# Per-head mean squares from split operands, placement of the parts by transfers, and a later recurrence in a one-layer hybrid decoder block

## The reference

```
h = rmsnorm(x, norm_g);  proj = h @ w_in          # split into u, z, q, k, v, gates ...
y_lru: causal conv of u, gates r, i; a = exp(-8 r softplus(-lam)); b = sqrt(1-a^2) i xc
       h_t = a_t h_(t-1) + b_t;  y_lru = h * silu(z)
y_nsa: q (8 heads), k, v (2 heads): compressed, selected and window branches, sigmoid gates, * silu(z)
y_fox: 8 heads, softmax(q k / 8 + c_t - c_s) v, c = cumsum(log sigmoid(forget)), * silu(z)
       (every q and k is first RMS-normed over its 64 channels:
        q * rsqrt(mean(q*q over the head) + 1e-6) * gain)
out = x + concat(y_lru, y_nsa, y_fox) @ w_out
```

## Time and profile before

| | |
|---|---|
| median of 3 runs | 423.2 us (422.87 to 423.55) |
| the profiled execution, its own time | 423.57 us |
| its span, first to last instruction | 421.8 us |
| TensorE clock granted | full in the whole span |
| busy: PE, PEld, DVE, ACT, POOL | 413.2, 325.5, 285.7, 261.4, 62.5 us |
| projection of u to vn, of zl | about 9 to 107 us, 107 to 137 us |
| first attention stage | 137 to 206 us |
| fq to zn | 206 to 297 us |
| second attention stage | 297 to 337 us |
| zf and output projection | 329 to 422 us |

### The profile page before, as it was taken

The page is one execution under the profiler, slowest core; times in us unless marked ns, Lnnn a source line. Parts: engine busy times, 40 slices in busy tenths (PEclk is TensorE's granted clock), DMA queues, the critical chain, the costliest instruction groups (busy, mean ns, idle before and its releaser), DMA issues.

```text
span 421.8 us, 6567 instructions
## 1 busy us (share of the span) xinstructions
PE 413.2 (98%) x2234; PEld 325.5 (77%) x2234; DVE 285.7 (68%) x616; ACT 261.4 (62%) x519; POOL 62.5 (15%) x122
## 2 busy tenths in 40 slices
PE   8999999999999899999999999999799999999996
PEld 7876788779888766666677987988576688888885
DVE  4667759988998876766378756699777389422205
ACT  5846996687465887886088778771888554322200
POOL 3000000000000666564000000000466100000000
PEclk9999999999999999999999999999999999999999
DMA  8923534420313000000421234437710115731005
GB/s 283 343 78 101 165 99 113 135 68 35 101 51 102 0 2 1 2 1 2 135 86 55 101 82 121 124 109 167 198 33 2 51 59 196 278 101 66 2 0 199
DMA packets 14017, 40.51 MB, mean 96 GB/s; under 512 B 1928, under 2 KB 2184, under 8 KB 13728
## 3 DMA queue, kind: packets, MB, share of 16 engines
q1 hardware_dynamic: 13552, 39.51, 29.8%
q10 hardware_dynamic: 432, 0.58, 0.4%
HBM read 32.17 MB, written 2.10 MB: 81 GB/s over the span
## 4 chain that ended last, share of the span: by engine, by line
PE 77%; DVE 14%; issue 3%; ACT 2%; POOL 1%; SPq 1%; DMA 1%; POOLq 0%; DVEq 0%; ACTq 0%
PE bank L1425 10%; PE bank L1427 10%; PE bank L1426 10%; PE bank L1610 6%; PE bank L1591 6%; PE bank L1701 5%; PE bank L1700 5%; PE bank L1699 5%; PE bank L1581 3%; PE bank L1582 3%; PE bank L1500 2%; DVE wl L1000 2%; PE bank L1632 2%; PE bank L1398 2%; PE bank L1400 2%
## 5 line engine op out<-in xcount | busy, mean ns | idle before, releaser
L1425 PE MATMUL bank<-xh,wh 128*128 128x512 f32 x240 | 99.6, 415 | 0.0
L1427 PE MATMUL bank<-xh,wl 128*128 128x512 f32 x240 | 93.8, 391 | 0.0
L1426 PE MATMUL bank<-xl,wh 128*128 128x512 f32 x240 | 93.7, 390 | 0.0
L1000 DVE TENSOR_TENSOR wl<-raw,wh 128x1024 fp32r<-128x1024 f32 (+1 forms) x50 | 60.0, 1204 | 37.0 <-ACT wh L611 36.8
L611 ACT ACTIVATE wh<-raw 128x1024 fp32r<-128x1024 f32 (+1 forms) x50 | 51.6, 1037 | 30.4 <-PE bank L1701 25.9
L1425 PEld LDWEIGHTS bank<-xh,wh 128*128 128x128 f32 x240 | 45.1, 188 | 14.8 <-issue 5.4
L1224 DVE CUSTOM_DVE_ANT_0 bank<-bank,mask_row 128x256 f32<-128x256 f32 (+3 forms) x96 | 46.6, 499 | 13.4 <-PE bank L1582 13.2
L1426 PEld LDWEIGHTS bank<-xl,wh 128*128 128x128 f32 x240 | 45.1, 188 | 11.3 <-issue 2.6
L1427 PEld LDWEIGHTS bank<-xh,wl 128*128 128x128 f32 x240 | 45.0, 188 | 9.7
L588 POOL TENSOR_SCALAR probs<-probs,rcp,gates 128x384 f32<-128x384 f32 (+3 forms) x44 | 26.5, 613 | 135.4 <-DVE rcp L1244 135.3
L792 ACT ACTIVATE probs<-bank,negmax 128x256 f32<-128x256 f32 (+3 forms) x64 | 33.7, 530 | 6.2 <-DVE negmax L1224 5.9
(11 more groups left out here) (246 smaller groups left out, 769.1 us busy)
## 6 DMA issues: line engine op xcount, KB each, us to landing
raw<-in_w_in SPq DMA_DIRECT2D x35, 512.0 KB, 3.3
raw<-in_w_out SPq DMA_DIRECT2D x12, 512.0 KB, 3.4
x_raw<-in_xT SPq DMA_DIRECT2D x8, 256.0 KB, 6.1
x_res<-in_x_tok SPq DMA_DIRECT2D x1, 2048.0 KB, 10.1
out_y<-y_out SPq DMA_DIRECT2D x8, 256.0 KB, 2.1
raw<-in_w_in SPq DMA_DIRECT2D x3, 384.0 KB, 3.3
cmp_w_sb<-in_cmp_w SPq DMA_DIRECT2D x1, 1024.0 KB, 5.6
kh_fox<-kh_fox SPq DMA_DIRECT2D x8, 128.0 KB, 2.3
```

The lines of the kernel that those rows point to most:

```text
L1000: dve.tensor_tensor(wl[:, c % HL, cols], raw[:, c % RAW, cols], wh[:, c % HL, cols].bitcast(F32), ALU.subtract).then_inc(wl_ready, 1)
L1425: pe.matmul(dst, hi, xh[:, k, :], start=(k == 0), stop=False)
L1426: pe.matmul(dst, hi, xl[:, k, :], start=False, stop=False)
L1427: mm = pe.matmul(dst, lo, xh[:, k, :], start=False, stop=(k == KT - 1))
```

## The change

1. **Head means.** ACT copies the squares to an fp32r plane (its high part), DVE makes the low part in a second plane (`square_low`), and PE multiplies both by an fp32r block matrix (`block_r`), two fast matmuls instead of one fp32 product. The bank alternates. The place of the product moves from the middle of the next chunk (k = 5) to its last eighth (k = 7); in vn to token tile 1, k = 3; in vf behind token tile 1.
2. **Parts.** High and low part of a normed chunk are each one instruction of 128 partitions, into the same two planes as the squares. There are two such plane pairs (`parts_nsa`, then `parts_fox`), used in turn (n even, n odd). SP then places them by four transfers a chunk (`stack`), for queries too. ACT may write the squares of chunk n only when the four transfers of chunk n-2 have landed (`stacked`, one semaphore for even and one for odd n).
3. **Inverse root.** The fourth ACT instruction of the guess goes; gains carry the factor.
4. **Recurrence.** `TAIL_AT` is a table of three parts a step; most of it moves from the ks to vn chunks into the end of the first attention stage and the fox chunks. Two `lru_output` move to vf0.
5. **Weights.** vn0 and vn1 are split at nq1, vn2 at nq2; in the fox steps the split of squares comes first. `split_low` of zf1 moves from step zn2 to the end of the second attention stage.
6. **Forget rows.** `place_queries` of pair 1, all `place_c` and `place_queries` of pair 2 stand ahead of the load of the last input chunk.

```
@@ act: before(c), for c in NORMED
                     act.activation(sq[:, :], qr[:, n % 2, :], ACT.Square).then_inc(sq_ready, 1)
+                    act.wait_ge(sq_ready, n + 1)
+                    if n >= 2:
+                        act.wait_ge(stacked[n % 2], COPIES * (n // 2))
+                    act.activation(norm_parts(c)[:, 0, :], sq[:, :], ACT.Copy).then_inc(sq_high, 1)
@@ act: norm_high(c)
-                    for s in range(2):
-                        high, _ = operand_parts(c, s)
-                        act.activation(high, qr[half_of(s), n % 2, :], ACT.Copy).then_inc(h_ready, 1)
+                    act.activation(norm_parts(c)[:, 0, :], qr[:, n % 2, :], ACT.Copy).then_inc(h_ready, 1)
@@ new: COPIES = 4 * 16, and
+        def norm_parts(c):
+            n = nth_normed(c)
+            return (parts_nsa if n < NSA_NORMED else parts_fox)[:, 2 * (n % 2):2 * (n % 2) + 2, :]
@@ dve
+            def square_low(c):
+                if c in NORMED:
+                    parts = norm_parts(c)
+                    dve.wait_ge(sq_high, nth_normed(c) + 1)
+                    dve.tensor_tensor(parts[:, 1, :], sq[:, :], parts[:, 0, :].bitcast(F32),
+                                      ALU.subtract).then_inc(sq_low, 1)
@@ pe: head_mean(c)
-                pe.wait_ge(sq_ready, n + 1)
-                pe.matmul(MEAN[:, :], block_mean, sq[:, :], start=True, stop=True).then_inc(norm_mean, 1)
+                pe.wait_ge(sq_low, n + 1)
+                parts = norm_parts(c)
+                pe.matmul(norm_bank(n), block_r[:, :], parts[:, 0, :], start=True, stop=False)
+                pe.matmul(norm_bank(n), block_r[:, :], parts[:, 1, :], start=False, stop=True).then_inc(norm_mean, 1)
@@ pe: project(c)
-                    if k == KT // 2 + 1 and c - 1 in NORMED:
+                    if k == KT - 1 and c - 1 in NORMED:
                         head_mean(c - 1)
@@ sp: stack(c)
+                    if kind in ("nq", "fq"):
+                        copies = ((q[own, :], parts[own, 0, :]), (q[other, :], parts[own, 1, :]))
+                    elif kind == "fk":
+                        copies = ((k[own, :, :], parts[own, :, :]), (k[other, 0, :], parts[own, 0, :]))
+                    else:
+                        copies = ((k[own, :, :], parts[own, :, :]), (k[other, :, :], parts[own, :, :]))
+                    for dst, src in copies:
+                        sp.dma_start(dst.bitcast(F32), src.bitcast(F32)).then_inc(stacked[nth_normed(c) % 2], 16)
@@ pe: cmp_scores(0)
+                    if (t, h) == (0, HEADS - 2):
+                        wait_stacked(pe, NSA_NORMED)
@@ sp: the loop over chunks
                 if c == N_IN - 1:
-                    place_c(0)
+                    place_queries(1)
+                    for i in range(HEADS // 2):
+                        place_c(i)
+                    place_queries(2)
@@
-TAIL_AT = (AT["ks", 0], AT["kw", 0], AT["nq", 0], AT["nq", 1], AT["nq", 2], AT["vn", 0], AT["vf", 2], AT["vf", 2])
+TAIL_AT = {AT["ks", 0]: ((0, 0), (0, 1)), AT["vn", 0]: ((0, 2),), AT["fq", 0]: ((1, 2), (2, 0)), AT["fq", 1]: ((2, 1),),
+           AT["vf", 0]: ((2, 2),), AT["vf", 2]: ((3, 0), (3, 1), (3, 2))}
```

More of the change, by code:

```diff
@@ L521, in _ @@
                 if c == N_IN - 1:
-                    place_c(0)
+                    place_queries(1)
+                    for i in range(HEADS // 2):
+                        place_c(i)
+                    place_queries(2)
+                if c == N_IN:
+                    place_queries(3)
                 load_w(c)
-                if c == N_IN:
-                    for i in range(1, HEADS // 2):
-                        place_c(i)
-                        place_queries(i)
                 k = c - 5
@@ L601, in split_ahead @@
             def split_ahead(c):
-                if c + AHEAD != AT["vn", 2]:
-                    split(c + AHEAD)
+                for x in ahead(c):
+                    split(x)
             def split(c):
@@ L883, in _ @@
                     continue
+                if c in NORMED:
+                    before(c)
                 split_ahead(c)
@@ L886, in _ @@
                     lru_sigmoids(0)
-                before(c)
+                if c not in NORMED:
+                    before(c)
                 if c == AT["u", 3]:
                     lru_sigmoids(1)
-                if c + AHEAD == AT["vn", 1]:
-                    split(AT["vn", 2])
                 if c == AT["kc", 0]:
@@ L909, in _ @@
                 norm_seeds(c - 1)
-                if c < FOX_END - 1:
+                before(c)
+                read_tokens(c, 0, 1)
+                if c < FOX_END - 1 and c != AT["vf", 1]:
                     split(c + AHEAD)
-                before(c)
-                read_tokens(c, 0, MIDDLE)
+                read_tokens(c, 1, MIDDLE)
                 norm_high(c - 1)
@@ L916, in _ @@
                 if c == AT["vf", 0]:
+                    split(AT["vf", 1] + AHEAD)
                     lru_roots((LRU_T - 1,))
@@ L1279, in _ @@
             dve.tensor_scalar(csp[:, 0, :], csp[:, 0, :], 4.0, None, ALU.mult).then_inc(csp_ready, 1)
+            for first, n, scale in (("nq_g", 2, 64.0), ("ks_g", 3, 1.0)):
+                g = chn[:, CH[first]:CH[first] + n]
+                link(dve.tensor_scalar(g, g, -0.5 * scale, None, ALU.mult))
             dve.wait_ge(rms_seed, 1)
@@ L1325, in _ @@
                 if c >= 1:
+                    norm_root(c - 1)
+                square_low(c)
+                if c >= 1:
                     norm(c - 1)
-                if c + AHEAD != AT["vn", 2]:
-                    split_low(c + AHEAD)
+                for x in ahead(c):
+                    split_low(x)
                 if c >= 1:
                     low_parts(c - 1)
-                if c + AHEAD == AT["vn", 1]:
-                    split_low(AT["vn", 2])
                 if c == AT["nq", 3]:
@@ L1401, in project @@
                         mm.then_inc(proj_done, 1)
[L1402 removed]
+                        if kind == "vf" and t == 1:
                             head_mean(c - 1)
```

215 lines of the change are left out of this document (121 added, 94 removed).

## The result

| | before | changed |
|---|---|---|
| median of 4 runs | 423.38 us (422.87 to 423.69) | 436.41 us (436.25 to 436.63) |
| the profiled execution, its span | 423.57, 421.8 us | 436.25, 434.5 us |
| first unit of attention 1 waits for its exp, until | 138.40 us | 147.28 us |
| last matmul of zn3 | 296.40 us | 309.62 us |

The ratio is 1.031 (95% interval 1.030 to 1.032): slower by 13.0 us, where 9.0 had been forecast.

The account below looks back on a forecast made before the run. PE, busy 98%, was taken as the bound. Attention starting 7.4 us later, fox chunks +2.55 and second attention stage -1.0 gave 9.0 on 423.6: 432.5 profiled, 432.1 us median, range 422.5 to 435.5.

Parts of the forecast that it names:

- this loop: Squares' copy of n waits for transfers of n-2; one turn 8.05 us for queries against PE's 5.9 a chunk.
- L(0): End of low_parts of chunk 0 on DVE, forecast at 70.4 us, against 68.3 before.
- A - L, keys: From low_parts' end on DVE to ACT's squares copy two chunks later, for ks and kw: 6.6 us.
- A - L, queries: From low_parts' end on DVE to ACT's squares copy two chunks later, for queries: 4.3 us.
- A - L, fk: From low_parts' end to the squares copy two chunks later, for fk's four copies (768 KB): 5.4 us.
- L(n-1) - A(n): From the start of ACT's squares copy of n to the end of DVE's low_parts of n-1: 3.75 us.
- mean - A: From the start of ACT's squares copy to when PE can take that chunk's mean: 1.45 us.
- second attention stage and zf: PE's 1.3 us wait for placed queries goes, 0.3 comes at the first place_c: net -1.0 us.
- the price of the transfers: Four transfers, low_parts' end to squares copy: 4.3 us for queries, 6.6 for keys at half-partition rate.
- A (keys at full rate, 426.6): Rival: key transfers move as fast as weight loads, low bound 4.3 us; 426.6 us, chance 0.22.
- B (no bound, 416.5): Rival: transfers are no bound, the two planes suffice and the kernel gets faster; 416.5 us, chance 0.14.
- C (split mean no cheaper): Rival: on PE the split mean costs as much as the fp32 one, two weights being loaded; 437.8 us, chance 0.04.

Follow-up runs that it names:

- own_planes: Changed kernel with the squares' parts in two planes of their own, so the squares' copy waits for no transfer; 417.48 us, ratio 0.987.
- fifth_transfer: Changed kernel with the last of each normed chunk's four transfers issued as two of half the columns, same bytes; 437.8 us, ratio 1.034.
- keys_half_bytes: Changed kernel with the transfers of ks and kw carrying the high plane alone, low planes zero; 430.84 us, ratio 1.018.
- after_fp32_mean: Changed kernel with the mean one fp32 product again and no parts of the squares; 422.57 us, ratio 0.998.
- before_split_mean: Kernel before with the split mean alone, squares' parts in two planes of their own; 431.3 us, ratio 1.020.
- filler_matmuls: Changed kernel with 18, 10 and 6 extra matmuls while PE waits for the squares of n = 2, 9 and 13; 435.86 us, ratio 1.030.
- early_low_parts: Changed kernel with DVE making the low parts of chunk n-1 ahead of the low part of the next weights; 434.6 us, ratio 1.027.
- keys_alternate_halves: Changed kernel with the four key transfers reordered so queue neighbours read different halves of the partitions; 436.36 us, ratio 1.031.

## Why the prediction was wrong, and where it was right

Right were the sign, the mechanism and the place: ACT's copy waits for transfers at n = 2 to 5, 8 to 10 and 13, PE's gaps stand ahead of six of those means, and own_planes shows that nothing but this loop makes the kernel slower. The sums of all three stages ran low, by 0.5 to 1.8 us, and the range (422.5 to 435.5) ended 0.9 below the measured 436.4. Term by term:

| term | forecast | measured |
|---|---|---|
| L(0) | 70.4 | 70.81 |
| A - L, keys | 6.6, twice | 7.07, 7.00 |
| A - L, queries, n = 4, 5, 8 | 4.3 | 4.26, 4.25, 4.28 |
| A - L, queries, n = 9, 10 | 4.3 | 4.69, 5.07 |
| A - L, fk | 5.4 | 5.67 |
| L(n-1) - A(n) | 3.75 | 3.83 |
| the same at n = 3, with two weight splits | 4.35 | 4.44 |
| mean - A | 1.45 | 1.48 |
| mean of n = 5 | 105.25 | 106.70 |
| second attention stage and zf | -1.0 | -0.54 |

**The failed step is the price of the transfers**, the term A = L + 6.6 for keys and A = L + 4.3 for queries. For the keys it was 7.07 and 7.00, and 0.87 of the 1.45 us at n = 5 come from there, 0.41 from L(0). Issuing isn't what binds (fifth_transfer). The trace shows two things that the term did not have. The keys alone moved at 195 GB/s (72 to 74 us), not 213. And the next weight load, issued at 74.02 while the keys still move, shares the DMA engines: from 70.8 to 77.8 us they moved 1.36 MB (194 GB/s over 7.0 us), of which the keys are 1.05. How the missing 0.4 to 0.5 us divide between the two was not tried. In the fox chunks n = 8 came as forecast, counted from the stage's start (232.73 against 232.89); n = 9 was 0.6 late, n = 10 1.5 and n = 13 1.8, mostly because the four transfers of fq1 and fq2 took 0.4 and 0.8 us longer than those of fq0, and those of fk 0.3 longer than forecast. I had one price for all queries; why theirs differ stays open (last section). Together: 8.95 (the unrounded sum) + 1.5 (up to attention 1) + 1.8 (fox) + 0.45 (behind) = 12.7, the difference of the profiled executions.

The waits themselves came out otherwise than listed (4.3, 0, 1.0, 1.8 for the forecast 3.8, 1.3, 2.7, 1.8), and this was no error of the loop: PE at the lower clock spent in matmuls what it would have waited. The sum over a taut loop does not see it.

**Rivals.** A (keys at full rate, 426.6) is refuted by the landing of 4.3 us and by keys_half_bytes. Of the two rules of the Trainium skill that were weighed, the measurement sides with "SBUF — State Buffer, Door 1: The DMA port swizzle", whose asymptote for half the partitions is about 218 GB/s: from 72 to 74 us, with the transfers of ks alone under way, the trace shows 195 GB/s, and from 72 to 77, with a part of the weight load in it, 220. The Trainium skill's other rule (DMA: Bandwidth & Descriptors, Anatomy of one DMA) would land 256 KB in an estimated 2.6 us; that section gives it for transfers issued by GpSimd, and these are SP's. B (no bound, 416.5) is what own_planes reached, 417.5: the planes, not the transfers, were short. C (split mean no cheaper) is refuted: 5.1 us between after_fp32_mean and own_planes.

**What I had set at nothing.** Neither ACT nor DVE gets more to do, I wrote, and left it there. True of the sum of the edits, but own_planes loses 1.6 us without the merged parts and 1.8 without the later recurrence, and before_split_mean, without these and the smaller differences named there, loses 8.1 against the kernel before. In the changed kernel both are in place, and the loop leaves DVE idle besides.

## What to carry to other kernels

When buffers in rotation are shared by two uses, one of which is freed by transfers, write the cycle down (write, issue, land, wait, the work up to the next write) and hold its time against the bounding engine's pace; if it is longer, the loop is the bound, and a gain on that engine is lost in it. Ask first which of the two uses really needs the slow release: here 4 KB a partition for the short-lived squares turned a loss of 13 us into a gain of 5.7. And an error in one term of such a loop is paid again in every turn: here the sums of three stages all erred to the same side, so a range needs the sum of the errors.

## What was not expected of the hardware

PE was granted the lower clock behind gaps of 4.3 us (79.4 to 88.7) and 2.5 us (242.5 to 245.7), but not behind those of 1.0 to 1.8 us; in keys_half_bytes, though, the clock was 0.63 from 94 to 96 us and 0.51 from 96 to 98, behind a wait of 1.5 us that ended at 92.86. In a taut loop it cost nothing that the medians could tell (filler_matmuls); with slack behind it some 1.4 us (n = 9 to 10 in early_low_parts), which filler matmuls ahead of n = 9 gave back.

Four transfers of 128 KB took 2.39 us in SP's queue for fq0 and fq3, 2.63 for fq1 and 3.13 for fq2, in own_planes alike (2.39, 2.64, 3.11), yet 2.38 for fq2 in filler_matmuls. The time in the queue is not all of it: in keys_alternate_halves fq2 took 2.38 there, and still A(10) came 5.28 us behind L(8). What makes them slower was not tried and stays open.
